# A two-layer block on one core: the second layer's last norm and its first query blocks by token tile, and less work placed ahead of the first gathered row

## Chip, core and metric

One core of one Trainium2 chip runs the whole kernel. The metric is device time in microseconds (us) of one execution. TensorE is written PE, VectorE DVE, ScalarE ACT, GpSimd POOL, and the engine that issues the plain loads SP.

## What is computed

Two transformer-like layers, one after the other, over 512 tokens of width 1024, in float32. The first is a hybrid of a gated delta rule and sparse attention with a gated feed-forward. The second has a convolution and pooling mixer, and then a layer of product-key experts (`peer`). This change lies around the start of `peer`:

```python
h2 = rmsnorm_2(x, norm2_g) * (1.0 + scale2) + shift2
def chunk_fn(hc):                                  # one tile of 128 tokens
    q = (hc @ w_query).reshape(PEER_CHUNK, 8, 256)         # 16 blocks of 128
    s1 = jnp.einsum('chk,nk->chn', q[..., :128], keys_1)   # even blocks
    s2 = jnp.einsum('chk,nk->chn', q[..., 128:], keys_2)   # odd blocks
    v1, i1 = lax.top_k(s1, 16); v2, i2 = lax.top_k(s2, 16)
    ...                                            # top 16 of the 256 sums
    u = jnp.take(expert_u, experts, axis=0)        # 16 rows a token and head
    act = jax.nn.gelu(jnp.einsum('chkd,cd->chk', u, hc))
    v = jnp.take(expert_v, experts, axis=0)
    return jnp.einsum('chk,chkd->cd', gate * act, v)
```

## The kernel before, in words

The tokens lie as `xT` (features on partitions, 512 tokens on columns). The second half of the kernel works on the first 256 tokens (half 0) and the last 256 (half 1). Half 0 runs ahead: by the time its `peer` layer starts, half 1 still has most of the first layer's feed-forward, and the whole mixer of the second layer, to do. That work of half 1 is laid beside the gathered rows of half 0.

**The rows.** A tile is 128 tokens; there are 4 tiles, 8 heads, 16 rows for each: 512 gathers. One gather brings 128 rows (one for each token) of 8 KB, u and v together, so 1.05 MB, into one of 9 slots of `ring_e` (`RING = 9`). POOL issues them in order; gather g waits until row g-9 has been added up. For each row DVE makes the dot product of u with the token's `hrow` (`row_dot`), ACT makes the weight of it (`weigh_pair`), and for the first two tiles ACT scales v and PE adds it by turning it into two banks (`add_turned` in `row_pair`, 8 turnings a row). The rows listed in `SIDE` are added by DVE instead. A step p is a pair of rows, so 256 steps. `p` 0 to 63 is the first tile.

**The routing.** `route(r, j)` on DVE has 16 pieces j that find the 16 experts of head r from its two blocks of key scores; the last piece writes `ecur`, for which POOL waits. Routes 0 and 1 run as a whole before the first row, route r+2 is spread over the 16 rows of head r.

**The queries.** `query(s, m)` is block m of half s on PE (8 products of 256 columns, each in two passes, so 16 records in the trace). ACT copies it (`keep_query`), PE makes the key scores (`key_scores`), ACT copies them (`keep_scores`). Route r of tile 0 needs blocks 2r and 2r+1. The first `EARLY` blocks stand ahead of the rows, the rest are put beside steps by `QUERY_AT[0]`.

**The weights.** All weights of this part (`w2`) come through three slots in one order, `ORDER`, made by `weight_order()`: the load of block t is issued by SP when PE is through with block t-3. A block is 512 KB. `expand` is a block of the first layer's feed-forward for half 1, its taps (`up_tap` on ACT, `expanded` on DVE) follow it; the first three stand ahead of the rows (`EARLY_UP = 3`), the others beside steps by `UP_AT`.

**Ahead of the first row**, PE in order:

```python
expand(0, 0, KT // 2)
pe.wait_ge(sq3_used, KT)
mm(PS[:, 5, :HF], ones, ssum3).then_inc(sq3_used, 1)   # the norm's sum
expand(0, KT // 2, KT)
expand(1)
query(0, 0)
...
```

ACT takes the root (`root3`), DVE the reciprocal and the eight products (`norm3`), ACT scale and shift (`apply3`), all over 256 columns. `turn_rows` turns the normed tokens of a tile so that they lie as rows (`hrow`), two halves a tile. DVE copies those of tile 0, ACT those of tile 1.

## Time and profile before

| | |
|---|---|
| median of 3 runs | 2406.8 us (2406.3, 2406.8, 2411.0) |
| the profiled execution | 2411.3 us |
| its span, first to last instruction | 2409.6 us |
| first gather issued | 923.9 us from the span's start |
| last gather issued | 2382.6 us |
| busy: PE, DVE, ACT, POOL | 87%, 69%, 36%, 26% |
| memory read | 750.6 MB, mean 313 GB/s over all |

The profiled execution's own time is 1.7 us above its span (launch and end). All times below are from the span's start. The 16 DMA engines of the core move some 420 GB/s at most in this trace, so a gather of 1.05 MB fills them for 2.5 us and a weight block of 0.52 MB for 1.25 us.

### The profile page before, as it was taken

Reading aid. Unit: us, or ns where it says so; the run is one execution under the profiler, and the core shown is the slowest. Engines: PE = TensorE matmul, PEld = TensorE weight load, DVE = VectorE, ACT = ScalarE, POOL = GpSimd, SP = SyncE. Lnnn points to the kernel's source line nnn. Section 1 sums busy time; section 2 is a strip of 40 time slices with the busy share of each in tenths; the row PEclk is TensorE's granted clock in tenths of the full one; section 3 lists DMA queues with packets and bytes.
Section 4 is the critical chain, followed back from the end, with each engine's and each line's share of the span. In section 5 each row is a group of like instructions: output and inputs, shape, how many; then the busy total and the mean of one; then the engine's idle time right before and its main releaser. Section 6 shows DMA issues by size and latency. Waiting matters only on the chain.

```text
span 2409.6 us, 26622 instructions
## 1 busy us (share of the span) xinstructions
PE 2090.4 (87%) x8894; PEld 1490.4 (62%) x8894; DVE 1665.0 (69%) x3729; ACT 871.7 (36%) x2126; POOL 636.9 (26%) x606
## 2 busy tenths in 40 slices
PE   7999998899999998999986898777688977777776
PEld 3444787788888887777775786677644423333332
DVE  5553645466647737989988898976676666676654
ACT  2321344521103214323325565357633333332322
POOL 2100000000010002333344334334444433444342
PEclk9999998999999999999998999899899999999999
DMA  8631120266784447999999999999999999999997
GB/s 346 200 123 52 36 69 2 96 213 239 245 307 135 137 150 311 404 417 416 412 416 420 419 411 418 391 395 420 420 420 421 421 421 421 421 416 421 422 409 307
DMA packets 131791, 754.33 MB, mean 313 GB/s; under 512 B 14544, under 2 KB 14672, under 8 KB 65616
## 3 DMA queue, kind: packets, MB, share of 16 engines
q0 software_dynamic: 87456, 588.90, 60.0%
q1 hardware_dynamic: 44208, 163.84, 18.8%
q8 instruction: 67, 1.10, 0.2%
q14 instruction: 60, 0.49, 0.1%
HBM read 750.59 MB, written 2.10 MB: 312 GB/s over the span
## 4 chain that ended last, share of the span: by engine, by line
PE 45%; DMA 32%; DVE 13%; ACT 6%; issue 3%; POOL 0%; DVEq 0%; SPq 0%; ACTq 0%; POOLq 0%
PE PS L605 43%; DMA arena<-experts_dram,ecur 25%; DVE arena L2652 4%; DVE arena L1921 3%; DMA ring<-up_dram 3%; DMA ring<-down_dram 2%; DVE h_all L1921 2%; PE PS L1160 2%; ACT L1786 1%; DMA ring<-w_out_dram 1%; ACT arena L1796 1%; ACT arena L1790 1%; DVE arena L1915 1%; DMA ring<-branch_dram 1%; ACT const L1798 1%
## 5 line engine op out<-in xcount | busy, mean ns | idle before, releaser
L605 PE MATMUL PS<-h_all,ring 128*128 128x256 f32 (+2 forms) x3584 | 894.6, 407 | 20.4 <-DMA ring<-up_dram 8.3
L2844 POOL DMA_INDIRECT arena<-experts_dram,ecur x512 | 587.6, 1148 | 1085.4 <-PE PS L1160 365.9
L2652 DVE CUSTOM_DVE_ANT_0 arena<-arena 128x1024 f32<-128x1024 f32 x512 | 625.7, 1222 | 292.2 <-DMA arena<-experts_dram,ecur 289.6
L605 PEld LDWEIGHTS PS<-h_all,ring 128*128 128x128 f32 x3584 | 679.3, 192 | 211.4 <-issue 104.2
L605 PE MATMUL PS<-arena,const 128*128 128x512 f32 (+1 forms) x1056 | 498.9, 620 | 133.8 <-ACT const L1798 124.9
L605 PEld LDWEIGHTS PS<-arena,const 128*128 128x128 f32 x1056 | 198.5, 196 | 418.2 <-issue 217.6
L1160 PE MATMUL PS<-const,arena 128*128 128x128 f32 x1304 | 190.8, 302 | 108.9 <-ACT arena L1796 105.6
L1786 ACT ACTIVATE arena<-arena 128x2 f32<-128x2 f32 x255 | 51.6, 202 | 636.6 <-DVE arena L2652 636.2
L605 PE MATMUL PS<-arena,ring 128*128 128x256 f32 x1088 | 245.8, 384 | 13.3 <-DMA ring<-down_dram 8.0
L1160 PEld LDWEIGHTS PS<-const,arena 128*128 128x128 f32 x1304 | 167.5, 156 | 133.2 <-ACT arena L1796 115.9
L605 PEld LDWEIGHTS PS<-arena,ring 128*128 128x128 f32 x1088 | 206.0, 192 | 47.6 <-DMA ring<-down_dram 13.5
L1796 ACT ACTIVATE arena<-arena 128x1024 f32<-128x1024 f32 x161 | 177.6, 1134 | 0.0
L605 PE MATMUL PS<-arena 128*128 128x128 f32 (+4 forms) x936 | 138.5, 300 | 8.5 <-ACT arena L1566 3.4
L605 PEld LDWEIGHTS PS<-arena 128*128 128x128 f32 (+2 forms) x936 | 118.6, 195 | 28.9 <-issue 12.8
L1921 DVE SCALAR_TENSOR_TENSOR arena<-arena 128x1024 f32<-128x1024 f32 (+3 forms) x132 | 125.6, 952 | 2.4
L1972 DVE CUSTOM_DVE_ANT_0 arena<-arena 128x1024 f32<-128x1024 f32 x92 | 109.1, 1222 | 24.8 <-DMA arena<-ada_dram 23.4
L1790 ACT ACTIVATE arena<-arena 128x1 f32<-128x1 f32 x510 | 122.3, 287 | 8.4
L1921 DVE SCALAR_TENSOR_TENSOR arena<-PS,param,arena 128x255 f32<-128x255 f32 (+3 forms) x128 | 72.2, 564 | 42.4 <-ACT arena L1406 31.5
L1921 DVE SCALAR_TENSOR_TENSOR xT<-PS,mod,xT 128x256 f32<-128x256 f32 x71 | 34.2, 482 | 85.1 <-PE PS L605 84.4
L1798 ACT ACTIVATE const<-const,arena 128x128 f32<-128x128 f32 x254 | 86.2, 387 | 0.0
L2824 POOL DMA_DIRECT2D arena<-crow_dram x1 | 0.5, 531 | 319.3 <-ACT arena L1570 319.3
L2831 POOL DMA_DIRECT2D arena<-ada_dram x44 | 23.4, 531 | 221.9 <-DVE mod L1972 209.1
(281 smaller groups left out, 1683.1 us busy)
## 6 DMA issues: line engine op xcount, KB each, us to landing
ring<-up_dram SPq DMA_DIRECT2D x88, 512.0 KB, 5.1
ring<-w_in_dram SPq DMA_DIRECT2D x80, 512.0 KB, 4.2
arena<-ada_dram POOLq DMA_DIRECT2D x80, 512.0 KB, 5.1
ring<-w_out_dram SPq DMA_DIRECT2D x32, 512.0 KB, 4.5
ring<-query_dram SPq DMA_DIRECT2D x32, 512.0 KB, 7.9
ring<-down_dram SPq DMA_DIRECT2D x16, 704.0 KB, 5.9
ring<-branch_dram SPq DMA_DIRECT2D x16, 512.0 KB, 6.1
arena<-experts_dram,ecur POOLq DMA_INDIRECT x512, 15.0
```

Of the source, the lines that this page charges most:

```text
L605: return nc.tensor.matmul(o, l, r, start=start, stop=stop)
L1160: ins = nc.tensor.matmul(PS[:, k // 4, (k % 4) * P:(k % 4 + 1) * P], row[:, k * P:(k + 1) * P], ident, start=start and k % 4 == 0, stop=st ...
L1786: A(wts[:, b, :], dots[:, b, :], ACT.Gelu_apprx_tanh).then_inc(gelu_ready, 1)
L1790: A(wts[:, b, k:k + 1], wts[:, b, k:k + 1], ACT.Copy, scale=gcur[:, r % 3, j:j + 1]).then_inc(w_ready2, 1)
L1796: A(row, row, ACT.Copy, scale=wts[:, b, k:k + 1]).then_inc(row_scaled, 1)
L1798: A(diag[:, b, k, :], ident, ACT.Copy, scale=wts[:, b, k:k + 1]).then_inc(diag_ready if k == rows[-1] else act_step, 1)
L1915: return V.tensor_tensor(out=o, in0=x, in1=y, op=op)
L1921: return V.scalar_tensor_tensor(out=o, in0=x, scalar=s_, in1=y, op0=op0, op1=op1)
L1972: V.tensor_tensor_reduce(out=w, in0=w, in1=row, scale=1.0, scalar=0.0, op0=MUL, op1=ADD, accum_out=mod[:, blk, t:t + 1]).then_inc(used, 1)
L2652: V.tensor_tensor_reduce(out=u, in0=u, in1=hrow[:, (r // HEADS) % 2, :], scale=1.0, scalar=0.0, op0=MUL, op1=ADD, accum_out=dots[:, p % NB ...
L2831: pool.dma_start(ring_2[:, j, :], a["ada_2"][bass.ds(i * SLOTS + j, 1)].rearrange("o p n -> p (o n)")).then_inc(slot_2_ready[j], 16)
L2844: nc.gpsimd.indirect_dma_start(out=ring_e[:, g % RING, :], out_offset=None, in_=a["experts"], in_offset=bass.IndirectOffsetOnAxis(ap=ecur[ ...
```

## The change

Half 0's last norm is done for each tile of 128 tokens instead of for 256 columns at once: root, reciprocal, products, scale and shift of tile 0, then those of tile 1 (`root_tile`, `norm_tile`, `apply_tile`). Query blocks 0 and 1 are made by tile too, and their key scores with them (`query_tile`, `key_scores_tile`), so that route 0 can start on the scores of tile 0 alone. Only query blocks 0 to 5 stay ahead of the rows; 6, 7 and 8 stand at steps 0, 2 and 4. `expand(1)` comes after the queries, next to `expand(2)`. DVE makes their taps after the second row's dot product. ACT copies tile 0's turned rows. Tile 1 is turned at steps 48 and 51.

```diff
-EARLY = 8
+EARLY = 6
-QUERY_AT = [{m: 1 + 3 * (7 * (m - EARLY) + 3) // 5 for m in range(EARLY, 16)},
+QUERY_AT = [{m: (0, 2, 4)[m - EARLY] if m < 9 else 1 + 3 * (7 * (m - 8) + 3) // 5 for m in range(EARLY, 16)},
...
-    order += [("w_out_2", 0, m) for m in range(KT)] + [("up", 1, 0), ("up", 1, 1)]
-    order += [("query", 0, m) for m in range(EARLY)] + [("up", 1, 2)]
+    order += [("w_out_2", 0, m) for m in range(KT)] + [("up", 1, 0)]
+    order += [("query", 0, m) for m in range(EARLY)] + [("up", 1, 1), ("up", 1, 2)]
...
+            def query_tile(m, c):
+                w = weights("query", 0, m)
+                t = slice(c * P, (c + 1) * P)
+                for k in range(KT):
+                    if m == 0:
+                        pe.wait_ge(h3_ready, KT * c + k + 1)
+                    ins = mm(PS[:, bank("query", 0, m), t], w[k], hv[:, 0, k, t], k == 0, k == KT - 1)
+                ins.then_inc(half_done if c else first_queries, 1)
+            def key_scores_tile(c):
+                t = slice(c * P, (c + 1) * P)
+                if c:
+                    pe.wait_ge(sc2_ready, c)
+                for m in range(2):
+                    pe.wait_ge(q_ready, 2 * c + m + 1)
+                    ins = mm(PS[:, 6, m * P:(m + 1) * P], qT[:, m, t], mat("keys2") if m else mat("keys1"))
+                ins.then_inc(sc2_done, 1)
...
                 if start:
-                    pe.wait_ge(hr_ready, 4)
+                    pe.wait_ge(hr_ready, 2 if p == 0 else 4)
...
             expand(0, KT // 2, KT)
-            expand(1)
-            query(0, 0)
-            query(0, 1)
-            key_scores(0, 0)
+            for c in range(2):
+                query_tile(0, c)
+                query_tile(1, c)
+                key_scores_tile(c)
+            query(0, 2)
+            query(0, 3)
+            key_scores(0, 2)
             turn_rows(0, 0, 0)
             turn_rows(0, 1, 1)
-            key_scores(0, 1)
-            turn_rows(1, 0, 7)
-            pe.wait_ge(hr_ready, 1)
-            turn_rows(1, 1, 0)
-            query(0, 2)
-            for m in range(3, EARLY):
-                query(0, m)
-                key_scores(0, m - 1)
+            key_scores(0, 3)
+            query(0, 4)
+            query(0, 5)
+            key_scores(0, 4)
+            key_scores(0, 5)
+            expand(1)
             expand(2)
...
-                if 0 < c < NC - 1 and q == 48:
-                    pe.wait_ge(h3_ready, 3 * KT)
-                    pe.wait_ge(xrow_ready, 2 * c)
+                if c < NC - 1 and q == 48:
+                    if c:
+                        pe.wait_ge(h3_ready, 4 * KT)
+                        pe.wait_ge(xrow_ready, 2 * c)
                     turn_rows(c + 1, 0, 7)
-                if 0 < c < NC - 1 and q == 51:
+                if c < NC - 1 and q == 51:
...
+            def root_tile(c):
+                t = slice(c * P, (c + 1) * P)
+                act.wait_ge(sq3_used, SUMS3[1])
+                A(rs3[:, t], PS[:, 5, t], ACT.Sqrt, bias=eps, scale=1.0 / D).then_inc(std3_ready, 1)
+            def apply_tile(c, lo, hi):
+                t = slice(c * P, (c + 1) * P)
+                act.wait_ge(mod_ready, 4)
+                for k in range(lo, hi):
+                    act.wait_ge(normed3, KT * c + k + 1)
+                    h = hv[:, 0, k, t]
+                    A(h, h, ACT.Identity, bias=mod[:, 1, 24 + k:25 + k], scale=eff[:, 3, k:k + 1]).then_inc(h3_ready, 1)
...
-            root3(0)
+            root_tile(0)
+            root_tile(1)
+            apply_tile(0, 0, KT)
             up_tap(0)
-            apply3(0)
+            apply_tile(1, 0, 2)
+            keep_query_tile(0, 0)
+            apply_tile(1, 2, 5)
+            keep_query_tile(1, 0)
+            keep_scores_tile(0)
+            apply_tile(1, 5, KT)
...
+            keep_rows(0, 0, 0)
+            keep_rows(0, 1, 1)
+            exp_gates(0)
...
+            exp_gates(1)
             up_tap(1)
...
-            norm3(0)
+            norm_tile(0)
+            norm_tile(1)
             expanded(0)
-            expanded(1)
...
-                    dve.wait_ge(sc2_ready, 16 * (c // 2) + (2 * h + 2 if c % 2 == 0 else 16))
+                    dve.wait_ge(sc2_ready, 16 * (c // 2) + (2 * h + 2 if c % 2 == 0 else 16) if r else 1)
...
+                if p == 0:
+                    expanded(1)
+                    expanded(2)
...
-            for t in range(2):
-                dve.wait_ge(hr_done, t + 1)
-                copy(hrow[:, 0, t * S:(t + 1) * S], PS[:, t, :]).then_inc(hr_ready, 1)
...
-            expanded(2)
```

PE's order from the norm's sum (the row with `ring,const`) to the first gathered rows. `h_all,ring` with 258 columns is `expand`, with 256 or 128 a query block; `mats,arena` are key scores, `const,h_all` turns tokens, `const,arena` adds a gathered row (8 a row). Before:

```order
L605 MATMUL PS<-h_all,ring 128x258 x12
L605 MATMUL PS<-h_all,ring 128x256 x16
L605 MATMUL PS<-mats,arena 128x128 x2
L1153 MATMUL PS<-const,h_all 128x128 x8
L605 MATMUL PS<-mats,arena 128x128 x2
L1153 MATMUL PS<-const,h_all 128x128 x8
L605 MATMUL PS<-h_all,ring 128x256 x16
```

Now:

```order
L610 MATMUL PS<-h_all,ring 128x258 x4
L610 MATMUL PS<-h_all,ring 128x128 x16
L610 MATMUL PS<-mats,arena 128x128 x2
L610 MATMUL PS<-h_all,ring 128x128 x16
L610 MATMUL PS<-mats,arena 128x128 x2
L610 MATMUL PS<-h_all,ring 128x256 x16
L610 MATMUL PS<-mats,arena 128x128 x2
L1178 MATMUL PS<-const,h_all 128x128 x8
```

The whole `expand(1)` (8 of the 12) is gone from the front, the first key scores stand behind half of the two query blocks, and one of the two turnings is gone.

PE beside the first steps, from the last `expand` ahead of the rows. Before:

```order
L605 MATMUL PS<-h_all,ring 128x258 x8
L1160 MATMUL PS<-const,arena 128x128 x16
L605 MATMUL PS<-mats,arena 128x128 x2
L1160 MATMUL PS<-const,arena 128x128 x8
L605 MATMUL PS<-h_all,ring 128x258 x16
L1160 MATMUL PS<-const,arena 128x128 x8
L605 MATMUL PS<-h_all,ring 128x256 x8
L605 MATMUL PS<-h_all,ring 128x258 x8
L1160 MATMUL PS<-const,arena 128x128 x8
L605 MATMUL PS<-h_all,ring 128x258 x24
L1160 MATMUL PS<-const,arena 128x128 x8
```

Now:

```order
L1185 MATMUL PS<-const,arena 128x128 x16
L610 MATMUL PS<-h_all,ring 128x256 x8
L1185 MATMUL PS<-const,arena 128x128 x8
L610 MATMUL PS<-h_all,ring 128x258 x16
L1185 MATMUL PS<-const,arena 128x128 x8
L610 MATMUL PS<-h_all,ring 128x256 x8
L610 MATMUL PS<-h_all,ring 128x258 x8
L1185 MATMUL PS<-const,arena 128x128 x8
L610 MATMUL PS<-mats,arena 128x128 x2
L610 MATMUL PS<-h_all,ring 128x258 x8
L610 MATMUL PS<-h_all,ring 128x256 x8
L610 MATMUL PS<-h_all,ring 128x258 x16
```

Between the rows of step 0 and the row of step 5 (the last line of the first piece; in the second it follows directly) stood seven blocks, and now there are nine.

SP's order of loads from the first block of the feed-forward on. Before:

```order
L590 DMA ring<-up_dram 128x1024 x2
L590 DMA ring<-query_dram 128x1024 x8
L590 DMA ring<-up_dram 128x1024 x3
L590 DMA ring<-query_dram 128x1024
L590 DMA ring<-up_dram 128x1024 x7
```

Now:

```order
L595 DMA ring<-up_dram 128x1024
L595 DMA ring<-query_dram 128x1024 x6
L595 DMA ring<-up_dram 128x1024 x2
L595 DMA ring<-query_dram 128x1024
L595 DMA ring<-up_dram 128x1024 x2
L595 DMA ring<-query_dram 128x1024
L595 DMA ring<-up_dram 128x1024 x2
```

The number of loads is the same; three blocks (two of queries and one of the feed-forward) have moved from ahead of query block 5's load to behind it or into the rows.

## Rows read from the trace of the kernel before

**Rows 1.** The page: the span, and GB/s in 40 slices of it

```profile
span 2409.6 us, 26622 instructions
...
GB/s 346 200 123 52 36 69 2 96 213 239 245 307 135 137 150 311 404 417 416 412 416 420 419 411 418 391 395 420 420 420 421 421 421 421 421 416 421 422 409 307
```

**Rows 2.** Windows: busy us of each engine, PEclk, DMA share, GB/s

```profile
914.50:923.50 9.00, 9.00 (x47) 8.02 (x46) 8.44 (x36) 2.24 (x5) 0.00 (x0) 1.00 0.30 92
970.00:980.00 10.00, 10.00 (x51) 8.75 (x51) 8.27 (x14) 4.77 (x11) 5.35 (x4) 1.00 0.96 342
927.50:2390.00 1462.50, 1190.70 (x4768) 808.54 (x4766) 1124.43 (x2625) 613.81 (x1564) 584.67 (x509) 0.95 1.01 416
```

**Rows 3.** Timeline of POOL: gathers 0, 9, 15 and 19

```profile
923.94 1.00 POOL L2844 DMA_INDIRECT arena<-experts_dram,ecur  x1 [213.29 <-DVE ecur L1924]
...
951.95 0.94 POOL L2844 DMA_INDIRECT arena<-experts_dram,ecur  x1 [17.02 <-PE PS L1160]
...
973.74 0.94 POOL L2844 DMA_INDIRECT arena<-experts_dram,ecur  x1 [7.82 <-PE PS L1160]
...
985.08 1.74 POOL L2844 DMA_INDIRECT arena<-experts_dram,ecur  x1 [4.57 <-PE PS L1160]
```

**Rows 4.** Timeline of DVE: norm, copies of tile 0, starts of routes 0, 1 and rows

```profile
900.73 1.75 DVE L2494 RECIPROCAL rs<-rs 128x256 f32<-128x256 f32 x1 [1.37 <-ACT rs L1690]
902.52 2.77 DVE L1915 TENSOR_TENSOR h_all<-xT,rs 128x256 f32<-128x256 f32 x8
...
914.55 0.29 DVE L2572 MAX8 arena<-arena 128x8 f32<-128x128 f32 x1
...
926.67 0.29 DVE L2572 MAX8 arena<-arena 128x8 f32<-128x128 f32 x1 [3.01 <-ACT arena L1717]
...
943.71 1.23 DVE L2652 CUSTOM_DVE_ANT_0 arena<-arena 128x1024 f32<-128x1024 f32 x1
```

**Rows 5.** Timeline of ACT: scale and shift, a query block's copy, the first weighing

```profile
903.04 4.04 ACT L1700 ACTIVATE h_all<-h_all,mod,eff 128x256 f32<-128x256 f32 x8 [0.57 <-DVE h_all L1915]
...
912.29 0.38 ACT L1712 ACTIVATE arena<-PS 128x256 f32<-128x256 f32 x1 [3.07 <-PE PS L605]
...
946.55 1.28 ACT L1786 ACT_TABLE_LOAD   x1 [3.92 <-DVE arena L2652]
```

**Rows 6.** Timeline of PE: blocks ahead of the rows, and beside the first steps

```profile
899.95 12.30 PE L605 MATMUL PS<-h_all,ring 128*128 128x258 f32 x56
...
913.86 1.04 PE L1153 MATMUL PS<-const,h_all 128*128 128x128 f32 x8
...
938.27 3.76 PE L605 MATMUL PS<-h_all,ring 128*128 128x258 f32 x16
949.74 3.64 PE L1160 MATMUL PS<-const,arena 128*128 128x128 f32 x16 [7.71 <-ACT arena L1796]
...
968.84 3.75 PE L605 MATMUL PS<-h_all,ring 128*128 128x258 f32 x16 [1.92 <-DMA ring<-up_dram]
...
983.77 1.03 PE L1160 MATMUL PS<-const,arena 128*128 128x128 f32 x8
```

**Rows 7.** Timeline of PE around 406: products of 128 columns, two a pair

```profile
406.26 1.47 PE L605 MATMUL PS<-arena 128*128 128x128 f32 x10
```

**Rows 8.** DMA issues, count, size, median us to landing: 899 to 927.5, then 927.5 to 2390

```profile
ring<-query_dram SPq DMA_DIRECT2D x7, 512.0 KB, 3.3
...
ring<-up_dram SPq DMA_DIRECT2D x42, 512.0 KB, 8.4
```

**Rows 9.** Gathers 15, 19 and 21 (issued 973.74, 985.08, 994.36): us from issue to landing

```profile
DMA to landing us min/median/max: 7.5/7.5/7.5
...
DMA to landing us min/median/max: 11.1/11.1/11.1
...
DMA to landing us min/median/max: 9.4/9.4/9.4
```

**Rows 10.** Windows around PE's idle time ahead of the first rows

```profile
942.00:945.00 3.00, 0.03 (x1) 0.00 (x0) 2.26 (x5) 0.56 (x1) 0.00 (x0) 0.98 1.02 416
945.00:955.00 10.00, 5.26 (x25) 5.29 (x26) 9.96 (x32) 7.25 (x14) 1.88 (x2) 0.50 1.01 420
```

More of the change, by code:

```diff
@@ L465, in build @@
         q_ready = sem("q_ready")
+        first_queries = sem("first_queries")
         qkv_ready = sem("qkv_ready")
@@ L534, in evicted, with query_kept @@
                 return x2_ready, KT + m + 1
-            return q_ready, 16 * half + m + 1
+            return query_kept(half, m)
+        def query_kept(half, m):
+            return q_ready, 16 * half + m + 3
         def score_banks(n):
@@ L1709, in keep_query, with keep_query_tile, keep_scores_tile @@
                 act.wait_ge(half_done, TURN["query", s, m] + 1)
-                if 16 * s + m >= 2:
-                    act.wait_ge(sc2_done, 16 * s + m - 1)
+                act.wait_ge(sc2_done, max(2, 16 * s + m - 1))
                 A(qT[:, m % 2, :], PS[:, bank("query", s, m), :HF], ACT.Copy).then_inc(q_ready, 1)
+            def keep_query_tile(m, c):
+                t = slice(c * P, (c + 1) * P)
+                act.wait_ge(half_done if c else first_queries, TURN["query", 0, m] + 1 if c else m + 1)
+                A(qT[:, m, t], PS[:, bank("query", 0, m), t], ACT.Copy).then_inc(q_ready, 1)
+            def keep_scores_tile(c):
+                act.wait_ge(sc2_done, c + 1)
+                A(sS[:, 0, c, 0, :, :], PS[:, 6, :HF].rearrange("p (z n) -> p z n", n=NKEYS), ACT.Copy).then_inc(sc2_ready, 1)
             def keep_scores(s, m):
@@ L1721, in keep_rows @@
                 act.wait_ge(hr_done, 2 * c + half + 1)
-                act.wait_ge(hr_ready, 2 * c + half)
+                if c + half:
+                    act.wait_ge(hr_ready, 2 * c + half)
                 if c > 1:
@@ L1743, in _ @@
                 square_block(0, k)
[L1744 removed]
+            root_tile(0)
+            root_tile(1)
+            apply_tile(0, 0, KT)
             up_tap(0)
[L1746 to L1760 removed]
+            apply_tile(1, 0, 2)
[4 more added lines that the diff above has]
+            apply_tile(1, 5, KT)
+            keep_query_tile(0, 1)
+            keep_query_tile(1, 1)
+            keep_scores_tile(1)
+            keep_query(0, 2)
+            keep_query(0, 3)
+            keep_scores(0, 2)
+            keep_scores(0, 3)
+            keep_rows(0, 0, 0)
+            keep_rows(0, 1, 1)
+            exp_gates(0)
+            keep_query(0, 4)
+            keep_query(0, 5)
+            keep_scores(0, 4)
+            keep_scores(0, 5)
+            exp_gates(1)
+            up_tap(1)
             up_tap(2)
@@ L1884, in beside @@
                     deviation(FIN_AT[p - 2])
-                if 0 < c < NC - 1 and q == 50:
+                if c < NC - 1 and q == 50:
                     keep_rows(c + 1, 0, 7)
-                if 0 < c < NC - 1 and q == 53:
+                if c < NC - 1 and q == 53:
                     keep_rows(c + 1, 1, 7)
@@ L2489, in add_block, with norm_tile @@
                 stt(o, PS[:, bank("w_out_2", s, m), :HF], gate_q[:, m:m + 1], o, MUL, ADD).then_inc(x3_ready, 1)
+            def norm_tile(c):
+                t = slice(c * P, (c + 1) * P)
+                dve.wait_ge(std3_ready, c + 1)
+                V.reciprocal(rs3[:, t], rs3[:, t]).then_inc(vec_step, 1)
+                dve.wait_ge(vec_step, n(vec_step))
+                dve.wait_ge(x3_ready, KT)
+                for k in range(KT):
+                    tt(hv[:, 0, k, t], xT[:, k, t], rs3[:, t], MUL).then_inc(normed3, 1)
             def norm3(s):
-                dve.wait_ge(std3_ready, s + 1)
+                dve.wait_ge(std3_ready, s + 2)
                 V.reciprocal(rs3, rs3).then_inc(vec_step, 1)
```

29 lines of the change are left out of this document (5 added, 24 removed).

## The prediction

> **What bounds the kernel now.** I read the page's slices first. From the seventeenth slice on the core moves 391 to 422 GB/s, and before that never more than 346 [rows 1]. The windows say it sharply: from 927.5 to 2390 us the DMA share is 1.01 and the rate 416 GB/s, while DVE is busy 1124 of 1462 us and PE 1191 [rows 2]. Just ahead of the rows it is 92 GB/s [rows 2]. So the last 1462 us are one stream of transfers, as long as it never runs dry; three things can shorten the kernel there: that the stream starts earlier, that it has fewer bytes left when it starts, and that it has fewer gaps. The timeline of POOL shows the start, gather 0 at 923.94 [rows 3]. The timelines of DVE, ACT and PE show what leads to it: reciprocal and products, scale and shift, query blocks 0 and 1 with turnings, copies of the turned rows, then route 0 at 914.55, which takes 9.4 us to the gather [rows 3, 4]. One gap stands out: 342 GB/s between 970 and 980 [rows 2], when gather 15 came late at 973.74 after a wait of 7.82 us for PE [rows 3]. It landed in 7.5 us, the following ones in 9.4 and 11.1 [rows 9]; I read 7.5 as a queue that had run empty, and what is above it as rows still in line.
>
> **Change 1: the first gather.** The norm's sum is untouched, so ACT's root comes as before and the reciprocal starts at about 900.6. At 256 columns it takes 1.75 us; at 128 between 0.88 and 1.75, and I take 0.9. The first product follows after 0.3. Scale and shift runs at 4.04/8 = 0.505 us each [rows 5]; at 128 columns between half and all of it, I take 0.4, so tile 0 is through at 901.8 + 8 x 0.4 = 905.0. PE's first tile ends with it; the second needs 16 records. Pairs of 128 columns were issued every 0.147 us (1.47 over 10) [rows 7], so 2.35 us, 907.6. ACT meanwhile makes a tap (0.57, as the taps of the trace) and five applications, with copies of 0.3, until 908.2. Key scores 0.5, ACT's copy 0.4 [rows 5]: route 0 starts at 909.3 and not 914.55, 5.3 us earlier. Of this, 1.3 us are the two copies of turned rows that DVE no longer makes. With every halved instruction as dear as a whole one the gain is 3, with every one at half price 7. Gather 0 then stands at 918.6.
>
> TensorE's order holds one price against this: a product of 128 columns costs more than half of one of 256. Blocks of 256 columns take 3.46 us (12.30 over 56 records is 0.22 each, 16 a block) [rows 6]; two tiles take 4.7. That is 1.2 us more a block, but route 0 sees only the first tile. The Trainium skill, "TensorE: Matmul & The Clock Gate", section "LDWEIGHTS (loading the stationary operand)", gives the weight load by its columns alone, some 107 ns, whatever moves past it. By that a tile would take at least 1.7 us, against the 2.35 that I use from the row; the sum would be 0.6 us better at most.
>
> **Change 2: bytes left behind.** By gather 0, SP had issued 9 blocks from the first feed-forward block on (two of them, and queries 0 to 6). By 918.6 it will have issued seven: one, and queries 0 to 5. Two whole blocks, and some 0.3 of the one under way, are left to the full stream, at 0.52 MB and 416 GB/s 1.26 us each: 2.8 us, between 2.5 and 3.8. The stream's lead is therefore 5.3 - 2.8 = 2.5 us. If the gap of 970 to 980 does not come back, 10 x (416 - 342)/416 = 1.8 us more: 4.3.
>
> **Change 3: PE at the first rows.** Whether gaps come depends on PE, which frees the slots. Ahead of the rows PE loses queries 6 and 7 (6.9) and a turning of 0.87 (8 records in 1.04, overlapping) [rows 6], and gains 2.4 for two tiled blocks and some 3.5 of waits for apply and copies, because `expand(1)` no longer covers the norm. Written out: half an `expand` to 901.7, tile 0 and its scores to 908.8, tile 1 to 914, two queries 921, scores and a turning 922.8, two queries and scores 931, two `expand` 937.9. It was 938.27 + 3.76 = 942.03 [rows 6]. ACT then makes the last tap and the first weighing; from the table load to PE's first row it was 946.55 to 949.74, 3.2 us [rows 5, 6], so with the tap PE starts rows at 941.8, 7.9 earlier. DVE is no obstacle: route 1 can start at 923.2 (it was 926.67), lasts 9, and dots begin at 933 instead of 943.71 [rows 4], though the third waits for the taps until about 940.
>
> From there to row 10, at step 5, PE has nine blocks instead of seven. 941.8 + 2.2 for two rows + 9 x 3.46 + three rows at 0.87 + scores 0.45 = 978.2. Weights come through three slots: a block lands 8.4 us after its load is issued in the full stream, where it took 3.3 before [rows 8], and two blocks between cover 6.9, with a row 7.8. That leaves waits of 0.6 to 1.5 twice, like the one of 1.92 at 968.84 [rows 6]: 980.0 against 983.77, a lead of 3.8.
>
> The clock takes some back. PE stood still from 942.03; the granted clock fell close to 945 and was 0.50 until 955, though PE worked again from 949.74 [rows 6, 10]. That level is 1.2 GHz, against 2.4 at 1.00. Now PE stands still from 937.9 to 941.8, 3.9 us; the fall came after some 2.9 us, so I count it in, and with it a block at half clock and 2.7 us. PE's lead at row 10 is then 1.1.
>
> **The sum.** What a gather has in line over 7.5 us is its cushion: 11.1 - 7.5 = 3.6 at gather 19, 9.4 - 7.5 = 1.9 at gather 21 [rows 9]. It grows by PE's lead and shrinks by the stream's: 3.6 + 1.1 - 4.3 = 0.4 and 1.9 + 1.1 - 4.3 = -1.3. So 1.3 us are lost in a new gap near gather 21 and 3.0 stay. Behind it the order is the same. Tile 1's turning at steps 48 and 51 costs PE 0.9 us and ACT two copies of 512 columns; the cushion that hides it is larger there, and without one it is 2 us. `first_queries` and the other semaphores cost nothing that waits. The profiled execution took 2411.3 us, so its like would be 2408.3; it lies 4.5 above the median of the three, 2406.8, from which I count: 2403.8.
>
> **Rivals.** Two tenths of a per cent, 4.8 us, is about what a measurement of this kernel can tell from no change.
>
> *The full lead.* The clock does not fall, or weights come sooner. PE's lead is 3.8, gather 21 has 1.9 + 3.8 - 4.3 = 1.4 in hand, and all of 4.3 stays: 2402.5; with change 1 at its upper bound, up to 6: 2400.8. For it: waits of 1.92 us did not lower the clock. Chance 0.30, and a little over half of that passes 4.8. The Trainium skill, "DMA: Bandwidth & Descriptors", section "Queues, rings and completion order", has each DMA engine turn from queue to queue after every packet, so that a weight block would not stand behind gathers. It would then land in about as little as two shares of 1.26 us and the 2 or so of latency, the small waits for weights would go, and this rival would hold. The trace's 8.4 us speak against it.
>
> *Nothing left.* The first rows run at PE's pace. If PE reaches row 10 at 983.8 as before or 1 later, because the nine blocks wait for weights more than twice, the stream's lead is lost down to 0 or 1: 2406.3. For it: PE is busy 10 of 10 us in that stretch [rows 2]. Chance 0.17.
>
> *Slower.* The two query blocks are a debt of 6.9 us that PE has to work off at full load. It decides when row 10 comes later than 983.8 + 3.6 + the lead of 2.5, about 990: every us beyond is a us of dry stream. It takes weights landing in 11 us instead of 8.4, so that each of nine blocks waits 1.1 or more, and the later tiles of the feed-forward in turn. At 996 the price is 6: 2412. Against it: PE had short waits at 8.4, and loads get quicker when gathers are few. Chance 0.08.
>
> *The forecast*, 1.5 to 4 us faster, has 0.45; its own range is 2402.5 to 2405.5. The range of all, with no more than 2 in 10 outside, is 2400.8 to 2408.0. Faster by over 0.2% has 0.20 (from the full lead and the forecast's edge), within 0.2% 0.73, slower 0.07.
>
> **What would show it.** Gather 0 at 918 to 920, route 0 with no copies ahead of it; the first dot at 933 to 935, the third near 941; PE's first row at 941 to 943; the clock at 0.50 for some 5 us after it; row 10 between 979 and 984; GB/s above 400 in 970 to 980 and a dent near 985 to 1000; the last gather 3 us earlier. It is wrong if gather 0 gains less than 3, if row 10 comes after 985, or if a later gap (the clock's or the norms' of half 1) grows or closes by itself.

## The result and the profile after

The changed kernel takes 2411.64 us (median of 9 runs, 2409.21 to 2417.96), the kernel before beside it 2406.29 us (9 runs, 2405.70 to 2410.97). The ratio is 1.0020, with a 95% interval of 1.0011 to 1.0028: some 5 us slower, where 3 us faster were forecast. The profiled execution took 2413.53 us.

The page of the changed kernel (span, granted clock and GB/s in 40 slices):

```profile
span 2411.7 us, 26713 instructions
PEclk9999998999999999999998999898899999999999
GB/s 346 200 121 53 36 71 1 96 219 235 248 301 140 138 150 335 366 417 412 402 417 419 419 418 419 397 391 421 420 421 420 421 422 421 422 417 421 416 421 301
```

The sixteenth slice moves 335 GB/s and not 311, which is the earlier start; the seventeenth 366 and not 404, the twentieth 402 and not 412 [rows 1]. Windows of the changed kernel, columns as in [rows 2]; the last two are the stretches 28.5 to 110.5 and 110.5 to 300.5 us behind the start of the norm's sum:

```profile
924.00:932.00 8.00, 5.29 (x27) 4.29 (x26) 6.15 (x21) 1.57 (x6) 3.76 (x4) 1.00 1.01 423
970.00:980.00 10.00, 9.26 (x43) 7.76 (x41) 9.83 (x21) 3.45 (x9) 4.46 (x3) 1.00 0.94 354
980.00:990.00 10.00, 8.36 (x37) 7.10 (x38) 3.58 (x7) 2.75 (x7) 1.47 (x2) 0.83 0.79 302
990.00:1000.00 10.00, 10.00 (x53) 8.76 (x52) 8.88 (x25) 5.05 (x11) 3.19 (x3) 1.00 0.93 344
...
927.42:1009.42 82.00, 71.09 (x346) 60.53 (x345) 67.06 (x157) 33.03 (x79) 24.36 (x20) 0.96 0.96 381
1009.42:1199.42 190.00, 175.09 (x830) 147.31 (x830) 175.78 (x357) 62.80 (x159) 69.61 (x52) 0.98 1.01 411
```

The stream runs dry for 30 us on end, most of all at 302 GB/s between 980 and 990. Against 418 GB/s, 82 us at 381 are 7.3 us of dry stream, and 190 us at 411 are 3.2 more.

Timeline of POOL, gathers 0, 9, 15, 19 and 21 (answering to [rows 3]):

```profile
917.85 1.00 POOL L2909 DMA_INDIRECT arena<-experts_dram,ecur  x1 [207.68 <-DVE ecur L1980]
...
944.72 0.94 POOL L2909 DMA_INDIRECT arena<-experts_dram,ecur  x1 [15.89 <-PE PS L1185]
...
968.65 0.94 POOL L2909 DMA_INDIRECT arena<-experts_dram,ecur  x1 [6.26 <-PE PS L1185]
...
988.23 0.94 POOL L2909 DMA_INDIRECT arena<-experts_dram,ecur  x1 [13.16 <-PE PS L1185]
...
996.53 0.94 POOL L2909 DMA_INDIRECT arena<-experts_dram,ecur  x1 [5.66 <-PE PS L1185]
```

The gathers are 6.1, 7.2 and 5.1 us ahead of before's until gather 15. Gather 19 then waits 13.16 us for PE and comes 3.2 us later than in [rows 3]. The whole lead is lost there, and more.

Timeline of DVE (answering to [rows 4]):

```profile
900.10 0.95 DVE L2551 RECIPROCAL rs<-rs 128x128 f32<-128x128 f32 x1 [1.26 <-ACT rs L1716]
901.08 1.71 DVE L1971 TENSOR_TENSOR h_all<-xT,rs 128x128 f32<-128x128 f32 x8
...
908.45 0.29 DVE L2638 MAX8 arena<-arena 128x8 f32<-128x128 f32 x1 [2.14 <-ACT arena L1760]
...
928.56 0.28 DVE L1980 CAST arena<-pab 128x32 f32<-128x32 uint32 x1 [0.38 <-issue]
929.96 0.69 DVE L1971 TENSOR_TENSOR arena<-arena,const 128x512 f32<-128x512 f32 x1 [1.12 <-DVE arena L1980]
...
932.76 1.22 DVE L2718 CUSTOM_DVE_ANT_0 arena<-arena 128x1024 f32<-128x1024 f32 x1
```

Timeline of ACT: the eight scale and shift of tile 0, and the copies of query blocks 4 and 5:

```profile
901.47 3.19 ACT L1725 ACTIVATE h_all<-h_all,mod,eff 128x128 f32<-128x128 f32 x8 [1.22 <-DVE h_all L1971]
...
927.86 0.38 ACT L1749 ACTIVATE arena<-PS 128x256 f32<-128x256 f32 x1 [3.32 <-remote]
930.85 0.38 ACT L1749 ACTIVATE arena<-PS 128x256 f32<-128x256 f32 x1 [2.60 <-remote]
```

Timeline of PE, from the norm's sum to row 10 (answering to [rows 6]):

```profile
898.92 0.67 PE L610 MATMUL PS<-ring,const 128*128 128x256 f32 x2
...
902.11 4.87 PE L610 MATMUL PS<-h_all,ring 128*128 128x128 f32 x32 [0.78 <-ACT h_all L1725]
...
907.73 4.06 PE L610 MATMUL PS<-h_all,ring 128*128 128x128 f32 x32
...
921.16 7.07 PE L610 MATMUL PS<-h_all,ring 128*128 128x256 f32 x32
928.29 0.71 PE L610 MATMUL PS<-mats,arena 128*128 128x128 f32 x4
931.65 0.68 PE L610 MATMUL PS<-mats,arena 128*128 128x128 f32 x4 [2.64 <-ACT arena L1765]
932.17 7.37 PE L610 MATMUL PS<-h_all,ring 128*128 128x258 f32 x32
943.35 2.92 PE L1185 MATMUL PS<-const,arena 128*128 128x128 f32 x16 [3.81 <-ACT arena L1854]
946.06 4.41 PE L610 MATMUL PS<-h_all,ring 128*128 128x256 f32 x16
...
963.75 3.75 PE L610 MATMUL PS<-h_all,ring 128*128 128x258 f32 x16 [1.10 <-DMA ring<-up_dram]
...
981.64 5.44 PE L610 MATMUL PS<-h_all,ring 128*128 128x258 f32 x16 [2.38 <-DMA ring<-up_dram]
986.92 1.04 PE L1185 MATMUL PS<-const,arena 128*128 128x128 f32 x8
```

Two places are odd. At 931.65 two key scores wait 2.64 us for a copy of scores, which ACT makes right behind its copy of query block 5; that one it could only make at 930.85, though PE's own rows (whose ends are modelled) have the query blocks done some 3 us earlier. DVE stood still at the same time, in route 1: 0.38 us ahead of 928.56 and 1.12 ahead of 929.96, with nothing late that the trace names. From 924 to 932 PE is busy 5.29 us of 8. At 981.64 a block waits 2.38 us for its weights and then takes 5.44 us instead of 3.75, at a clock of 0.83 over that window. Row 10 stands at 986.92.

### The profile page after: what moved, and what is told of

Read it like the earlier page. It is cut to its first block, busy times and chain, and to the rows that moved or that the text cites. A ratio compares the mean times of both kernels' runs of the same rounds, so it can differ in the third digit from the quotient of the medians.

```text
span 2411.7 us, 26713 instructions
## 1 busy us (share of the span) xinstructions
PE 2094.9 (87%) x8926; PEld 1498.4 (62%) x8926; DVE 1664.8 (69%) x3736; ACT 874.2 (36%) x2139; POOL 632.1 (26%) x606
## 4 chain that ended last, share of the span: by engine, by line
PE 47%; DMA 31%; DVE 13%; ACT 6%; issue 3%; another core or an unknown queue 0%; POOL 0%; SPq 0%; DVEq 0%; ACTq 0%; POOLq 0%
PE PS L610 44%; DMA arena<-experts_dram,ecur 24%; DVE arena L2718 4%; DVE arena L1977 3%; DMA ring<-up_dram 3%; DMA ring<-down_dram 2%; PE PS L1185 2%; DVE h_all L1977 2%; ACT L1844 1%; ACT arena L1848 1%; ACT arena L1854 1%; DMA ring<-branch_dram 1%; DVE arena L1971 1%; ACT const L1856 1%; DMA ring<-w_out_dram 1%
## 5 line engine op out<-in xcount | busy, mean ns | idle before, releaser
L610 PE MATMUL PS<-h_all,ring 128*128 128x256 f32 (+3 forms) x3616 | 901.9, 407 | 23.9 <-DMA ring<-up_dram 11.0
L610 PEld LDWEIGHTS PS<-h_all,ring 128*128 128x128 f32 x3616 | 687.1, 194 | 214.8 <-issue 107.3
L1977 DVE SCALAR_TENSOR_TENSOR arena<-PS,param,arena 128x255 f32<-128x255 f32 (+3 forms) x128 | 72.2, 564 | 42.1 <-ACT arena L1431 31.2
L1977 DVE SCALAR_TENSOR_TENSOR xT<-PS,mod,xT 128x256 f32<-128x256 f32 x71 | 34.2, 482 | 85.4 <-PE PS L610 84.7
```

The lines of the kernel that those rows point to most:

```text
L610: return nc.tensor.matmul(o, l, r, start=start, stop=stop)
L1977: return V.scalar_tensor_tensor(out=o, in0=x, scalar=s_, in1=y, op0=op0, op1=op1)
```

## The experiments

Five groups of runs, no two on the same chip, each with the kernel before beside it. On which chip the first measurement ran isn't on record; it may be that of group 2. Since executions differ by up to 6 us before they come to the norm's sum, places are given below in us behind its start ("behind the sum"). "Dry" is what 28.5 to 110.5 us behind the sum miss of 418 GB/s, in us: 82 x (418 - rate)/418, with the rate of that window. Time is the median, the ratio is to the kernel before on the same chip, as the measurement gives it; the quotient of the two medians differs from it by up to 0.0006.

| run (group) | first dot, rows, row 10 | dry | time, ratio and 95% interval |
|---|---|---|---|
| the kernel before, its profile | 44.3, 50.3, 84.3 | 1.8 | |
| the changed kernel, its profile | 33.8, 44.4, 88.0 | 7.3 | 2411.64, 1.0020 (1.0011 to 1.0028) |
| e_repeat (1) | 32.3, 42.0, 82.7 | 1.4 | 2404.70, 0.9991 (0.9982 to 1.0000) |
| e_ahead8 (1) | 32.3, 50.7, 81.7 | 1.8 | 2405.75, 1.0000 (0.9991 to 1.0009) |
| e_q8_late (1) | 32.3, 42.1, 78.1 | 0.0 | 2405.44, 0.9991 (0.9982 to 1.0000) |
| e_only_early6 (1) | 38.1, 44.2, 84.6 | 0.0 | 2406.53, 0.9998 (0.9989 to 1.0007) |
| e_repeat2 (2) | 33.8, 47.1, 91.0 | 9.8 | 2411.51, 1.0019 (1.0009 to 1.0029) |
| e_warm (2) | 33.8, 47.1, 87.3 | 6.3 | 2408.39, 1.0001 (0.9992 to 1.0010) |
| e_ups_later (2) | 33.7, 45.8, 79.4 | 2.4 | 2406.38, 0.9993 (0.9984 to 1.0002) |
| e_both_later (2) | 33.7, 45.8, 70.9 | 1.6 | 2409.29, 1.0007 (0.9998 to 1.0016) |
| f_before (3) | 44.2, 50.2, 83.6 | 0.4 | 2408.05, 1.0003 (0.9994 to 1.0013) |
| f_repeat3 (3) | 32.3, 42.3, 82.8 | 1.6 | 2405.85, 0.9995 (0.9986 to 1.0005) |
| f_ahead8 (3) | 32.3, 50.6, 83.2 | 3.5 | 2406.61, 1.0002 (0.9993 to 1.0011) |
| f_only_early6 (3) | 38.1, 44.2, 85.1 | 0.4 | 2407.22, 1.0000 (0.9991 to 1.0009) |
| g_before2 (4) | 44.2, 50.2, 83.6 | 0.6 | 2407.75, 1.0006 (0.9997 to 1.0015) |
| g_repeat4 (4) | 32.3, 42.0, 82.9 | 2.0 | 2403.69, 0.9987 (0.9977 to 0.9996) |
| g_only_early6 (4) | 38.2, 44.2, 84.7 | 0.0 | 2406.19, 0.9996 (0.9987 to 1.0005) |
| g_ups_later (4) | 32.3, 42.0, 80.2 | 3.3 | 2407.23, 0.9999 (0.9990 to 1.0008) |
| h_q8_late (5) | 32.3, 42.1, 78.2 | 0.0 | 2405.04, 0.9988 (0.9979 to 0.9997) |
| h_only_early6 (5) | 38.1, 44.2, 84.7 | 0.0 | 2406.86, 0.9997 (0.9988 to 1.0006) |

**e_repeat: the changed kernel, unaltered, on a second occasion.**

> The changed kernel once more, unaltered. It tells whether the stop of PE between query block 4 and its scores (half_done seen 3 us late, 924 to 931 us), the wait of 2.4 us for weights before row 10 and the half clock at 982 us come every time. Both theories: 4 to 6 us over the kernel before; row 10 at 985 to 988 us, gather 0 at 918.

The timeline of PE in e_repeat:

```profile
896.62 0.67 PE L610 MATMUL PS<-ring,const 128*128 128x256 f32 x2
...
926.94 0.68 PE L610 MATMUL PS<-mats,arena 128*128 128x128 f32 x4 [0.56 <-ACT arena L1765]
927.46 7.30 PE L610 MATMUL PS<-h_all,ring 128*128 128x258 f32 x32
938.58 3.24 PE L1185 MATMUL PS<-const,arena 128*128 128x128 f32 x16 [3.81 <-ACT arena L1854]
941.61 4.03 PE L610 MATMUL PS<-h_all,ring 128*128 128x256 f32 x16
...
959.25 3.76 PE L610 MATMUL PS<-h_all,ring 128*128 128x258 f32 x16 [1.43 <-DMA ring<-up_dram]
...
975.70 3.75 PE L610 MATMUL PS<-h_all,ring 128*128 128x258 f32 x16 [0.95 <-DMA ring<-up_dram]
979.29 1.03 PE L1185 MATMUL PS<-const,arena 128*128 128x128 f32 x8
```

And the two windows in e_repeat, then the same stretches in f_before (the kernel before):

```profile
925.12:1007.12 82.00, 74.24 (x369) 63.77 (x368) 72.15 (x169) 34.40 (x79) 25.14 (x20) 0.98 1.01 411
1007.12:1197.12 190.00, 176.04 (x853) 147.85 (x851) 178.52 (x362) 64.53 (x164) 70.77 (x56) 1.00 1.02 417
```

```profile
927.35:1009.35 82.00, 72.01 (x353) 61.86 (x352) 72.80 (x178) 35.37 (x81) 26.28 (x24) 0.94 1.01 416
1009.35:1199.35 190.00, 175.92 (x846) 147.87 (x845) 178.14 (x363) 64.35 (x163) 68.60 (x53) 0.99 1.02 415
```

The same program, and it is 2.5 us faster than the kernel before beside it (2404.70 against 2407.21), not 5 slower. The key scores wait 0.56 us instead of 2.64, PE's rows come 42.0 us behind the sum instead of 44.4, the last block ahead of row 10 waits 0.95 us for weights and keeps its 3.75, and row 10 comes at 82.7 and not 88.0. The 5.3 us between them are 2.5 ahead of the rows; of the other 2.8, 1.4 are the longer last wait, 1.7 the half clock behind it and 0.4 the slower block at 946.06, with small shorter waits against them. I call what happens 26 to 31 us behind the sum the halt.

**e_repeat2, f_repeat3, g_repeat4: the changed kernel on three more occasions.**

> The changed kernel unaltered, on another occasion. Theory of the stops (the 5 us over the kernel before in the first measurement came from halts of PE in those executions, seen as products whose completion is counted 2.6 to 7 us late at nine or so places, which no other profile has): no halts in the profile, row 10 at 82 to 84 us behind the norm's sum, 2 to 3 us faster than the kernel before. Rival (the change makes the kernel prone to them): halts again, 3 to 6 us slower.

> The changed kernel, unaltered, for the third time. Theory: its time goes with the halt. Halted (first dot about 33.8 us and PE's rows 44.4 or later behind the norm's sum, row 10 at 87 or later): 3 to 6 us slower than before, ratio 1.0012 to 1.0025. Not halted (32.3, 42.0, 82.7): 2 to 3 us faster, ratio 0.9988 to 0.9992. Rival: the time is another by chance, and does not go with the three places.

> The changed kernel, unaltered, a fourth time. Halted (first dot 33.8 us, PE's rows 44.4 or later, row 10 at 87 or later behind the norm's sum): ratio 1.0012 to 1.0028. Not halted (32.3, 42.0, 82.7): ratio 0.9988 to 0.9996. Rival: the ratio does not go with the three places.

The two occasions with the halt (the first dot at 33.8) are at 1.0020 and 1.0019, the three without it at 0.9991, 0.9995 and 0.9987. No occasion mixed the two. The timeline of PE in e_repeat2 has the two expansions ahead of the rows, the first rows and the last block like this:

```profile
930.85 9.66 PE L610 MATMUL PS<-h_all,ring 128*128 128x258 f32 x32
...
944.33 3.65 PE L1185 MATMUL PS<-const,arena 128*128 128x128 f32 x16 [3.81 <-ACT arena L1854]
...
982.89 5.44 PE L610 MATMUL PS<-h_all,ring 128*128 128x258 f32 x16 [2.10 <-DMA ring<-up_dram]
```

The expansions took 9.66 us and not 7.37: here the clock fell right behind the halt already (0.75 on the mean of 931 to 941 us), and so the rows come at 47.1 and not at 44.4.

**f_before and g_before2: the kernel before, with profiles of its own.**

> The kernel before, unaltered, with a profile of its own on the chip on which the next three run. By the theory of the halt: if it shows none here (first dot 44.3 us and PE's rows 50.3 us behind the norm's sum, as before) while the changed kernel shows one, the halt belongs to the earlier gathers; if it shows one too, PE's rows and row 10 come about 3 us later than 50.3 and 84.3 us. Its time is the kernel before's, ratio 1.000.

> The kernel before, unaltered, on the chip of the changed kernel's fourth run. Theory: no halt that costs it anything on either kind of occasion (first dot 44.2, PE's rows 50.3, row 10 84 us behind the norm's sum). Rival: where the changed kernel is halted this one is too, and its row 10 comes at 87 or later.

Without a halt on either occasion they agree with each other within 0.1 us as far as row 10, and row 10 is 0.7 us earlier than in the first profile. Neither fell on a halting occasion, so they don't tell whether this kernel would be halted too.

**e_ahead8 and f_ahead8: query blocks 6 and 7 ahead of the rows again.**

```diff
-EARLY = 6
+EARLY = 8
-QUERY_AT = [{m: (0, 2, 4)[m - EARLY] if m < 9 else 1 + 3 * (7 * (m - 8) + 3) // 5 for m in range(EARLY, 16)},
+QUERY_AT = [{m: 1 + 3 * (7 * (m - 8) + 3) // 5 for m in range(EARLY, 16)},
```

> The changed kernel with query blocks 6 and 7 ahead of the rows again (and block 8 at step 2 as before), all else as changed. Debt theory (nine blocks instead of seven between the first rows and row 10 make the stream of gathers run dry): seven blocks again, rows start some 7 us later (950), row 10 at 984 or 985, loss of transfer between 960 and 1010 falls from 7.3 to 3 or 4 us, and the kernel is 1 to 3 us faster than the kernel before. Rival (the norm and queries by tile and the earlier start themselves cost, by collisions of gathers with PE's loads and stops): the loss stays, and the time stays 4 to 6 us over the kernel before.

> Query blocks 6 and 7 ahead of the first row again, block 8 at step 2, the rest as in the changed kernel. By the theory that what is left behind the first row is a debt which PE pays between rows 0 and 10: with a halt it comes to about the time of before (ratio 0.999 to 1.001), since row 10 has two blocks less ahead of it. By the rival, that the halt costs what it costs wherever the blocks lie: the same loss as the changed kernel, ratio 1.0012 or more.

Ratios 1.0000 and 1.0002: no gain of the earlier gather 0 by itself is shown (the medians lie 1.5 and 0.9 us under those of the kernel before, which the intervals of some 2 us each way don't tell from nothing). Timeline of PE and window of f_ahead8:

```profile
946.80 5.35 PE L1185 MATMUL PS<-const,arena 128*128 128x128 f32 x24 [3.81 <-ACT arena L1862]
```

```profile
946.00:952.00 6.00, 5.20 (x25) 5.23 (x26) 5.97 (x21) 4.18 (x10) 2.52 (x2) 0.50 0.65 231
```

Nine gathers start earlier, but PE frees the first slot at 50.6 us behind the sum as before, and by then the nine are through: 6 us at 231 GB/s, 2.7 us dry. The debt theory was not put to its test, since no halt came.

**e_only_early6, f_only_early6, g_only_early6, h_only_early6: the kernel before with its blocks 6, 7 and 8 at steps 0, 2 and 4, nothing by tile.**

```diff
-EARLY = 8
+EARLY = 6
-QUERY_AT = [{m: 1 + 3 * (7 * (m - EARLY) + 3) // 5 for m in range(EARLY, 16)},
+QUERY_AT = [{m: (0, 2, 4)[m - EARLY] if m < 9 else 1 + 3 * (7 * (m - 8) + 3) // 5 for m in range(EARLY, 16)},
```

> The kernel before with only query blocks 6, 7 and 8 moved to steps 0, 2 and 4 (norm, first queries, turnings and taps as before). Debt theory: gather 0 stays at 924, rows start 7 us earlier (943), row 10 within 2 us of 984 or later by the clock, so the move alone gains nothing and costs 0 to 3 us. Rival (the tile part costs): this kernel equals the kernel before or is faster by 1 to 3 us, since PE starts the rows earlier.

> The kernel before with query blocks 6, 7 and 8 alone moved to steps 0, 2 and 4; the norm and first blocks as before. If the halt comes with the tile part (gathers 6 us earlier), none here: PE's rows 44.2 us, row 10 84.6 us behind the norm's sum, ratio 0.9995 to 1.0005. If it comes with the occasion alone, PE's rows 47 and row 10 87 or later, ratio 1.001 or more.

> The kernel before with query blocks 6, 7 and 8 alone at steps 0, 2 and 4. Theory, that the halt needs the gathers 6 us earlier: PE's rows 44.2 and row 10 84.6 to 85.1 us behind the norm's sum on either kind of occasion, ratio 0.9995 to 1.0005. Rival, that the occasion alone brings it: PE's rows 47, row 10 87 or later, ratio 1.001 or more where the changed kernel is halted.

> The kernel before with query blocks 6, 7 and 8 alone at steps 0, 2 and 4, beside a kernel that has the tile part. If the halt needs the tile part: PE's rows 44.2 and row 10 84.6 to 85.1 us behind the norm's sum also where the other kernel is halted, ratio 0.9995 to 1.0005. If it comes with the occasion: PE's rows 47, row 10 87 or later there, ratio 1.001 or more.

0.9998, 1.0000, 0.9996, 0.9997: little or nothing either. PE's rows come 6 us earlier and the stream is next to never dry in the first 82 us, but gather 0 is still 24.5 us behind the sum and more bytes stand behind it. The two parts need each other; together they give 0.05% to 0.13%. By the means of the runs on the same chips, the changed kernel without a halt is 1.8 us under ahead8 (two chips, 95% interval 0.7 to 3.0) and 2.1 us under only_early6 (three chips, 1.3 to 2.9). All four fell on occasions on which nothing showed a halt.

**e_q8_late and h_q8_late: the queries left behind the first row spread further.**

```diff
-QUERY_AT = [{m: (0, 2, 4)[m - EARLY] if m < 9 else 1 + 3 * (7 * (m - 8) + 3) // 5 for m in range(EARLY, 16)},
+QUERY_AT = [{m: {6: 0, 7: 2, 8: 8, 9: 10, 10: 14, 11: 17, 12: 21, 13: 25, 14: 29, 15: 33}[m] for m in range(EARLY, 16)},
```

> The changed kernel with query block 8 at step 8 instead of 4, and 9 to 15 up to 3 steps later than they were. Debt theory: one block less before row 10, which comes 3.5 us earlier (983.5), 2 to 4 us less dry time, time 1 to 3 us over the kernel before or equal to it. Rival (the landing of weights and the clock set row 10, not the number of blocks): row 10 moves by less than 1.5 us, time as the changed kernel.

> The changed kernel with query block 8 at step 8 instead of 4 and blocks 9 to 15 at steps 10 to 33. With a halt (first dot 33.8 us behind the norm's sum instead of 32.3): row 10 at about 82 instead of 88 or later, ratio 0.9995 to 1.0005. Without one: row 10 at 78, gathers 6 us ahead of the kernel before, ratio 0.998 to 0.9992. Rival: further behind row 10 the blocks bring another dry stretch, and the ratio is no better than the changed kernel's 0.9987 to 0.9995 without a halt, and 1.0015 or more with one.

Row 10 is 4.5 us earlier and the stream is never dry there, and still the ratios, 0.9991 and 0.9988, are those of the changed kernel without a halt. Without one, then, PE's queue ahead of row 10 costs no more than 1 or 2 us. This is the version I would keep: it has 4.5 us in hand where the halt strikes. But no halting occasion came for it, so that this is worth anything there is not shown.

**e_warm: eight idle products of 256 columns into a free bank behind `expand(2)`,** so that PE doesn't stand still ahead of the rows.

```diff
+            for k in range(8):
+                mm(PS[:, 7, :HF], ident, const[:, 0:HF])
```

> The changed kernel with eight products of 256 columns that nobody reads (some 3.5 us of PE work) behind the last block ahead of the rows, so that PE does not stand idle there. Clock theory: the granted clock stays at 1.00 up to row 10, query block 6 takes 3.6 us instead of 4.0 to 4.4, row 10 comes 1 to 2 us earlier, and the time falls by up to 1 us, where the stream runs dry. Rival (the extra work delays the first row): row 0 later by 1 us or more and no gain.

Timeline of PE in e_warm:

```profile
939.76 3.61 PE L610 MATMUL PS<-const 128*128 128x256 f32 x16
943.74 2.04 PE L1185 MATMUL PS<-const,arena 128*128 128x128 f32 x16 [0.36 <-ACT arena L1856]
...
980.39 3.75 PE L610 MATMUL PS<-h_all,ring 128*128 128x258 f32 x16 [2.43 <-DMA ring<-up_dram]
```

On the same chip as e_repeat2, with the same halt and rows at 47.1 in both, row 10 is 3.7 us earlier and the time 3.1 us shorter (95% interval of the difference of medians 0.6 to 6.7). So the lower clock behind the first rows is worth about 3, of the 6 to 8 us that lie between the halted and the unhalted changed kernel (2411.5 against 2403.7 to 2405.9). The first two rows take 2.04 us and not 3.65. And the block behind the last wait keeps 3.75 us after a wait of 2.43, where it took 5.44 after 2.10 in e_repeat2.

**e_ups_later, g_ups_later: the expansions spread further; e_both_later: that and the later query blocks of e_q8_late.**

```diff
-    return 1 + 3 * (j + min(KT, (j + 3) // 6)) // 5
+    return 3 + 41 * (j + min(KT, (j + 3) // 6)) // 72
```

e_both_later has this edit and that of `QUERY_AT` shown for e_q8_late; it has no idle products.

> The changed kernel with the feed-forward blocks beside the steps starting at step 3 instead of 1, and at a slightly closer spacing to the same end. Debt theory (the changed kernel still loses 1 to 3 us of the stream between 28 and 300 us behind the norm's sum because PE has more than one and a half blocks a step): PE reaches row 10 six or more us earlier (three blocks less before it), no dry time, 1 to 2 us faster than the changed kernel. Rival (the stream is full anyway in the undisturbed case): same time as the changed kernel within 1 us.

> The feed-forward blocks from step 3 on and query block 8 at step 8. Debt theory: row 10 ten us earlier than in the changed kernel, the stream full up to 300 us, at best 2 us faster than the changed kernel. Rival: no more than one of the two alone, since a full stream can't be made fuller.

> The changed kernel with its feed-forward blocks' expansions spread further (3 + 41 x // 72). Theory, that PE's work between rows 0 and 10 is what the halt makes late: without a halt row 10 comes at 76 us or before behind the norm's sum, and the ratio is 0.998 to 0.9992 since no gather is taken back there; with one it is 79.4 and 0.999 to 1.0 as before. Rival, that the later expansions' taps only move the stall: ratio 0.9995 to 1.0005 without a halt.

With the halt e_ups_later gets 5.1 us back (2406.38 against 2411.51, interval 2.8 to 9.5), as less work ahead of row 10 should. Without it g_ups_later is no better than before, 0.9999, and against the changed kernel beside it 3.5 us worse (0.7 to 5.9). Timeline of PE in g_ups_later:

```profile
972.13 6.76 PE L610 MATMUL PS<-h_all,ring 128*128 128x258 f32 x16 [6.81 <-DVE ring L1977]
```

The later expansion finds its bank still taken by one whose taps DVE comes to late, PE stands 6.81 us, and the block behind takes 6.76 us instead of 3.75: the clock fell. That is the rival of its expectation, and it holds; row 10 came at 80.2, not at 76 or before. e_both_later has row 10 earliest of all, 70.9, and 1.0007: later query blocks and later expansions don't add up, and row 10 alone doesn't set the time. Why it is 2.9 us slower than e_ups_later I can't say; it has 5.0 us dry in the 190 us behind, against 1.8. Whether idle products and later expansions add up was not run.

## Why the prediction was wrong, point by point

**The first gather: right.** Reciprocal 0.95 us (forecast 0.9), scale and shift 3.19/8 = 0.40 (0.4). Taken from the sum, route 0 starts at 9.5 us (forecast 9.9) and gather 0 at 18.9 (19.2). The tiled blocks ran at 4.87/32 = 0.152 us a record and then at 4.06/32 = 0.127, where 0.147 was used. By the rule for weight loads in the Trainium skill, "TensorE: Matmul & The Clock Gate", section "LDWEIGHTS (loading the stationary operand)", 16 records are, as an estimate from it, at least 1.7 us; they took 2.0 to 2.4, which agrees.

**The bytes left behind: right.** Without a halt the sum closes: gather 0 is 5.6 us earlier behind the sum, 2.8 us of bytes go off that, the stream is as dry as in f_before (82 and 190 us at 411 and 417 GB/s against 416 and 415: 1.8 us in both), so 2.7 us faster should be left. The last instruction of e_repeat ends 1503.9 us behind the sum and that of f_before 1507.0: 3.1 us. In the changed kernel's first profile the windows add up to 10.5 us dry against 1.8; 2.8 - 8.7 = -5.9, and its end is at 1512.8, 5.8 us later than f_before's.

**The gap of 970 to 980: a term too large.** The prediction took it for a feature of the kernel and counted 1.8 us for its going. In f_before, the same kernel, the like stretch behind the sum moves 395 GB/s and not 342, and in g_before2 393:

```profile
969.40:979.40 10.00, 10.00 (x51) 8.76 (x50) 8.92 (x16) 5.01 (x12) 5.85 (x4) 1.00 1.01 395
```

That is worth some 0.5 us, so the lead of 4.3 us was 1.3 too much. By its own working 1.7 us would have been left without a halt; the means of the runs on the three chips without one give 2.6 (interval 1.8 to 3.4). That the forecast of 3.0 comes near is in part luck: the 190 us behind the first 82 are between 0.5 and 3.6 us dry in the profiles of both kernels without a halt, and no term had that.

**PE at the first rows: the step that failed.** It put the last `expand` at 937.9, rows at 941.8, row 10 at 982.7 and "PE's lead at row 10 is then 1.1". Measured: 939.5, 943.35, 986.92, a lead of -3.2. Nothing in it had PE and DVE stop without an operand that comes late. Where they don't stop the step is right to 0.6 us: in e_repeat the `expand` ends 38.1 us behind the sum (forecast 38.5), rows start at 42.0 (42.4), row 10 at 82.7 (83.3). Its overview, PE losing 7.8 us of work and gaining 5.9, doesn't fit the 4.1 us written out behind it; the trace has 4.4.

**The clock: a term of the wrong size, in the wrong place.** 2.7 us were counted for a fall around the first rows. The block behind them took 4.03 us in e_repeat and 4.41 in the changed kernel, against 3.62 at full clock: 0.4 to 0.8. The first two rows took 3.24 and 2.92 us, against 2.04 at full clock in e_warm, so it is 1.6 to 1.7 us in all. The dearer fall came at the last block, 1.7 us, behind a wait of 2.38, though the text argued that waits of 1.92 us did not lower the clock.

**Weights landing in 8.4 us: right without the halt.** The block of 975.70 in e_repeat was issued at 967.84 and landed in 7.8 us. In the changed kernel the like was issued at 972.35 and let PE go at 981.64, 9.3 us later. The timeline of SP there:

```profile
972.35 0.33 SPq L595 DMA_DIRECT2D ring<-up_dram  x1
```

In e_repeat, from 955 to 965 us, with both queues at work, gathers (q0) and loads (q1) moved nearly as many packets (packets, MB, share):

```profile
q0 software_dynamic: 388, 2.79, 67.9%
q1 hardware_dynamic: 368, 1.34, 33.2%
```

That agrees with the rule in the Trainium skill, "DMA: Bandwidth & Descriptors", section "Queues, rings and completion order", that the engines turn from queue to queue after every packet. The prediction read its 8.4 us as speaking against that rule, and there it was wrong; what failed was the landing of some 4.5 us that it worked out. The packets of the loads are half as long as those of the gathers (1.34 MB over 368 against 2.79 over 388), so the loads get a third of the bytes and not half: a block's 128 packets at 37 a us take 3.5 us. And the first packet comes late: the load issued at 945.67 in e_repeat has none before 948.9, that of 972.35 in the changed kernel none before 975.4. As an estimate, 3.2 and 3.5 us make 6.7 of the 7.8.

**The cushion: right in kind.** Without a halt it was right in size too: the new gap near gather 21, forecast at 1.3 us, is there. e_repeat issues gather 21 at 988.95 and moves 364 GB/s from 987.17 to 997.17, 1.3 us dry; f_repeat3 and g_repeat4 move 365 and 356 in the like stretch, f_before 419. With the halt the prediction's own formula with the measured lead gives 3.6 - 3.2 - 4.3 = -3.9 at gather 19 and 1.9 - 3.2 - 4.3 = -5.6 at gather 21: it would have said 4.3 - 5.6 = -1.3, slower. The two windows show 8.7 us more dry than f_before; 2 of it lie behind 110.5 us and were in no term. **The rival "slower" had the right mechanism,** a dry stream because row 10 comes late, but its point was set at 990. By its own cushions the kernel is slower from 983.8 + 1.9 = 985.7 on (gather 21) or 987.4 (gather 19); the stream's lead of 2.5 us was added on top, though the sum itself takes the stream's lead off the cushion. The stream ran dry with row 10 at 986.92.

**The order of the chances.** The forecast and the full lead held on three occasions of five. What the first occasion showed was no mishap of one run: the median of 9 runs there and that of 9 more of e_repeat2 are 5.4 and 4.3 us above before's.

**A slip in reading:** from the seventeenth slice on the rate is 391 to 422 GB/s only up to the last slice but one; the last has 307. Nothing hangs on it.

**What stays open.** What halts PE (about 3 us) and DVE (1.5 us) 26 to 31 us behind the sum on two occasions of six, and whether it needs the tile part. It falls when the nine first gathers fill the queues, but they do so without a halt too. The fetching of instructions was a suspicion. An instruction packet of 16 KB does lie where the halt lies, 26.8 to 27.2 us behind the sum in all 13 profiles with the tile part (at about 31 or later in those without), but it lies there and takes 1.0 us with a halt and without, so it alone doesn't explain one; it is neither shown nor ruled out. That the slow result comes from what the halt makes late rests on three things: the time goes with the halt on all five occasions of the changed kernel; its first profile ends 8.9 us later behind the sum than e_repeat's, of which the windows show 8.6 as dry stream; and e_warm and e_ups_later give back 3 and 5 us on a halted occasion. (e_warm's own profile is 2.6 us less dry than e_repeat2's, but ends as late, 1512.8 against 1512.5, so its gain rests on the medians alone.) The halt itself could not be put in or taken out, so something of the chip that brings both the halt and part of the loss is not excluded.

## What to carry to other kernels

An edit that starts the stream earlier and one that frees slots earlier were worth nothing alone and 1 to 3 us together: look for the second gap before the first is closed. When a change spends the slack of a queue, work out from which delay on it turns against you, and leave that much in hand: here row 10 coming 5 us later, or more, turned 2.5 us of gain into 5 us of loss. For gains of a tenth of a per cent, repeat the pair on several chips, with a profile each time: the ratio's interval on one chip, 1.0011 to 1.0028, did not cover what three others showed.
